# Fifth modulation vector moved behind the attention heads, and all six vectors on four column groups of TensorE

## The chip, the cores and the metric

The kernel runs on one NeuronCore of a Trainium2 chip. The metric is the device time of one execution in microseconds (us), the median of several runs; smaller is better. A profile is one further execution, recorded by the hardware profiler.

## The reference

Two layers (`DEPTH` = 2) of a backbone with model width 1024 run on 128 context tokens and 256 latent tokens, three tiles of 128 tokens. All is float32. What bears on the change is the modulation: two condition vectors (one for the context, one for the latent tokens) go through `silu` and a 1024 x 6144 matrix, and the six results of 1024 numbers each shift, scale and gate the layer.

```python
def modulation(cvec, w_mod_l, b_mod_l):
    m = jax.nn.silu(cvec) @ w_mod_l + b_mod_l
    return m.reshape(cvec.shape[0], 6, D_MODEL)

def trunk_layer(...):
    sh1, sc1, g1, sh2, sc2, g2 = [mod[:, i][:, None, :] for i in range(6)]
    h = rms_norm(x, n1) * (1.0 + sc1) + sh1
    proj = h @ w_in
    ...
    attn = block_attention(q, k_all, v_all)
    conv = conv_module(u, dw_w, dw_b, ln_g, ln_b)
    x = x + g1 * (jnp.concatenate([attn, conv], axis=-1) @ w_out)
    h2 = rms_norm(x, n2) * (1.0 + sc2) + sh2
    x = x + g2 * grouped_moe(h2, w_router, b_router, wg, wu, wd)
```

The vectors are counted from 0: vector 0 is `sh1`, vector 4 is `sc2` (the fifth), vector 5 is `g2`. Attention has 8 query heads and 2 key heads of width 64. The convolution has 31 taps on 512 channels (4 blocks of 128). The mixture has 16 experts.

## The kernel before, in words

Each engine has its program written out by hand (`block.tensor`, `block.vector`, `block.scalar`, `block.gpsimd`, `block.sync`), and the engines meet at semaphores. Nothing reorders the work: an engine does its instructions in the order of the code.

**Weights** come through a ring of eight slots of 2 MB in the tile `big`. SP issues all weight loads in one fixed order (`loads`), and each waits until TensorE has finished with what the slot held (`slot_used`). Per layer these are the vectors' weights (two pieces of 2 MB each), the input projection, the output projection, and three loads for each of 16 experts.

**A modulation vector** (`vector`, L1457) is eight steps k of the contraction. The stationary operand is `cs_rep[:, k, :]`, the two activated conditions repeated over 64 columns; the moving operand is one half (`LW` = 512 numbers) of the weight row. `LANES` = 2: one half goes to columns 0 to 63 of the array, the other to columns 64 to 127, so a vector is 16 matmuls of 64 columns x 512. The profile shows each float32 matmul as two records (and two weight loads), so a vector is 32 records. VectorE takes a vector out of PSUM (`mod_take`: L975 copies vectors 0 and 1, L979 adds the bias to 2, 3 and 5). `columns` (L1484) turns vectors 0 and 1 into columns by 16 small matmuls each. Vectors 2, 3, 4 and 5 are written to DRAM by GpSimd (`lane_out`, L323, one DMA for each lane) and read back broadcast to all partitions (`spread`, L547).

**Vector 4** goes another way: it is split over the eight heads (`HEAD_FILL`, `head_fill`, L1471). Every head has two of its 16 matmuls, with a stationary operand of 2 columns and 512 numbers moving; its first half (called 8) is done after head 3, its second (9) after head 7. VectorE takes each half with L983 and multiplies it by the gain of the second norm with L988, on two partitions. GpSimd writes it out with one DMA (L606).

**A head** on TensorE: for each tile the transposes of the probabilities (L1614) and the scores of the next head (L1590), then two matmuls of vector 4 (L1471), then probabilities times values (L1441, 128x64, 14 records). VectorE finds the maxima (L1176), does some convolution taps (L1102), and scales the head's output (L1182, L1184); ScalarE does the exponentials (L848) and takes the transposed probabilities (L855).

**The convolution's taps** are 124 VectorE instructions in one fixed order. `taps(n)` does the next n. The line that sets their places:

```python
EARLY_TAPS, ROPE_TAPS, BETWEEN_TAPS, LATE_TAPS, HEAD_TAPS = 80, 6, 6, 4, 4
```

80 come early, 6 inside each of the three rotary embeddings (`rope`; 6 after the first one in the second layer), 6 before `rope(1)`, 4 after vector 2 is taken: 108 ahead of the heads. The 16 that are left go 4 to a head, to heads 0 to 3.

**Behind the heads** TensorE transposes the convolution back (`conv_back`, L1601), transposes the heads' outputs (`mix_transposed`, L1647) and projects (`project_out`, L1662). Meanwhile the layer norm of the convolution runs through VectorE (L1192, L1197), GpSimd (L542, L543, L615, L616, L620) and ScalarE (L871). Its results let the second half of each `mix_transposed` go. Then comes the second norm, the router, the routing (VectorE, with vector 5 on TensorE beside it and, in the first layer, vectors 0 and 1 of the second), and the experts (L1746, L1762).

Of the kernel before, what the change touches and what calls it, by code (L numbers as in the profile page):

```python
# [5 lines left out]
ALU = mybir.AluOpType  # L6
# [30 lines left out]
LANES = 2  # L37
# [7 lines left out]
TAKES = [0, 1, 2, 3, 8, 9, 5]  # L45
# [81 lines left out]
EARLY_TAPS, ROPE_TAPS, BETWEEN_TAPS, LATE_TAPS, HEAD_TAPS = 80, 6, 6, 4, 4  # L127
# [100 lines left out]
def build(nc, x_prompt, x_sample, cache_k, cache_v, c, c_ctx, w_mod, b_mod, norm1_g, norm2_g, w_in, q_norm_g,  # L228
# [6 lines left out]
    with ExitStack() as ctx:  # L235
# [53 lines left out]
        assert o >= 5120 + 3 * LW  # L289
# [4 lines left out]
        sg = rowC = cut(CH)  # L294
# [67 lines left out]
        rowB_in = sem("rowB_in"); gain_in = sem("gain_in"); small_in = sem("small_in")  # L362
# [13 lines left out]
        mod_half_ps = sem("mod_half_ps")  # L376
# [152 lines left out]
        def _(pool):  # L529
# [25 lines left out]
            for l in range(LAYERS):  # L555
# [7 lines left out]
                pool.dma_start(rowS, b_mod[l:l + 1, 4 * D:5 * D].broadcast_to([2, D])).then_inc(rowB_in, 16)  # L563
# [34 lines left out]
                pool.wait_ge(modC_st, (l + 1) * 32)  # L598
# [30 lines left out]
                pool.wait_ge(modB_st, l * 48 + 48)  # L629
# [24 lines left out]
                pool.wait_ge(modG_st, (l + 1) * 32)  # L654
# [294 lines left out]
        def _(dve):  # L949
# [10 lines left out]
            def mod_take(l, c):  # L960

                bank = mod_bank(l, c)
                if c == 2:
                    dve.wait_ge(rowC_in, (l + 1) * 32)
                if c == 3:
                    dve.wait_ge(rowB_in, (l + 1) * 48)
                if c == 5:
                    dve.wait_ge(rowG_in, (l + 1) * 32)
                if c == 8:
                    dve.wait_ge(mod_half_ps, l + 1)  # L970
                else:
                    n = pieces(l, min(c, 4 if c == 9 else c))[-1][0]
                    dve.wait_ge(slot_used[slot_of(n)], uses(n))
# [3 lines left out]
                if c < 8:
                    row = (rowC[:, :], rowB, None, rowG)[c - 2]
                    v.tensor_tensor(row, ps[:, bank, :], row, ALU.add).then_inc(mod_taken, 1)  # L979
                else:  # L980
                    half = slice(c % 2 * SEG, (c % 2 + 1) * SEG)
                    row, gain = rowS[:, half], gainB[:, half]
                    v.tensor_tensor(row, ps[0:2, bank, :], row, ALU.add).then_inc(mod_taken, 1)  # L983
                if c in (8, 9):
                    if c == 8:
                        dve.wait_ge(gain_in, (l + 1) * 16)
# [42 lines left out]
            for l in range(LAYERS):  # L1029
# [142 lines left out]

# [258 lines left out]
        def _(pe):  # L1431
# [15 lines left out]
            def vector(l, j, k0=0, k1=KD):  # L1447

                for n, a, b in pieces(l, j):
                    for k in range(max(a, k0), min(b, k1)):  # L1450
# [5 lines left out]
                        for lane in range(LANES):  # L1456
                            mm = pe.matmul(ps[lane * LP:(lane + 1) * LP, mod_bank(l, j), :], cs_rep[:, k, :],  # L1457
                                           w[:, lane * LW:(lane + 1) * LW], start=(k == 0), stop=(k == KD - 1))
                        if k == b - 1:
                            mm.then_inc(slot_used[slot_of(n)], 1)  # L1460

            def head_fill(l, hd):

                c, k0, k1 = HEAD_FILL[hd]
                if k0 == 0:
                    pe.wait_ge(mod_taken, taken_at(l, 3 if c == 8 else 8))
                for n, a, b in pieces(l, 4):
                    for k in range(max(a, k0), min(b, k1)):
                        if c == 8 and k == a:
                            loaded(n)  # L1470
                        mm = pe.matmul(ps[0:2, mod_bank(l, c), :], cs_rep[:, k, 0:2],  # L1471
                                       slot_k(slot_of(n), b - a)[:, k - a, (c - 8) * SEG:(c - 7) * SEG],
                                       start=(k == 0), stop=(k == KD - 1))
                        if c == 8 and k == KD - 1:
                            mm.then_inc(mod_half_ps, 1)
                        if c == 9 and k == b - 1:
# [432 lines left out]
```

## Time and profile before

| what | us |
|---|---|
| runs: median (lowest to highest) of 3 | 1130.35 (1130.08 to 1140.29) |
| the profiled execution, its own time | 1134.84 |
| span in its trace | 1133.0 |
| TensorE busy in the span | 1003.9 (89%) |
| VectorE busy | 393.6 (35%) |
| granted TensorE clock, mean | 0.938 |

The span is the time from the first to the last instruction of the trace; the profiled execution's own time is 1.84 us longer. A granted clock of 1.00 is 2.4 GHz, 0.50 is 1.2 GHz. In the rows below PE is TensorE (PEld its weight loads), DVE is VectorE, ACT ScalarE, POOL GpSimd and SP the engine that issues the weight loads.

### The profile page before, as it was taken

Reading aid. Unit: us, or ns where it says so; the run is one execution under the profiler, and the core shown is the slowest. Engines: PE = TensorE matmul, PEld = TensorE weight load, DVE = VectorE, ACT = ScalarE, POOL = GpSimd, SP = SyncE. Lnnn points to the kernel's source line nnn. Section 1 sums busy time; section 2 is a strip of 40 time slices with the busy share of each in tenths; the row PEclk is TensorE's granted clock in tenths of the full one; section 3 lists DMA queues with packets and bytes.
Section 4 is the critical chain, followed back from the end, with each engine's and each line's share of the span. In section 5 each row is a group of like instructions: output and inputs, shape, how many; then the busy total and the mean of one; then the engine's idle time right before and its main releaser. Section 6 shows DMA issues by size and latency. Waiting matters only on the chain. (4 is left out here: it accounts for less than half of the span.)

```text
span 1133.0 us, 11425 instructions
## 1 busy us (share of the span) xinstructions
PE 1003.9 (89%) x4328; PEld 471.3 (42%) x4328; DVE 393.6 (35%) x857; ACT 152.3 (13%) x357; POOL 116.3 (10%) x176
## 2 busy tenths in 40 slices
PE   4799999999799998899899989999788888987993
PEld 1555544545233333333366534555433333333331
DVE  0159954334411111111035996434511111111106
ACT  1100144220000000000020014422000000000001
POOL 0100400501000000000111020050100000000001
PEclk9899989998899999999899999999689899999897
DMA  9926991259999996999980375235966999999814
GB/s 341 354 117 238 291 366 70 95 189 360 419 404 423 425 372 273 413 422 424 360 306 24 149 277 215 75 115 195 371 237 240 417 422 425 424 423 422 353 28 167
DMA packets 64406, 329.83 MB, mean 291 GB/s; under 512 B 6992, under 2 KB 9680, under 8 KB 47924
## 3 DMA queue, kind: packets, MB, share of 16 engines
q1 hardware_dynamic: 44224, 277.89, 61.2%
q0 software_dynamic: 8496, 28.68, 6.9%
q10 hardware_dynamic: 11588, 21.95, 5.9%
q8 instruction: 63, 1.03, 0.4%
q14 instruction: 35, 0.29, 0.1%
HBM read 306.67 MB, written 21.82 MB: 290 GB/s over the span
## 5 line engine op out<-in xcount | busy, mean ns | idle before, releaser
L1746 PE MATMUL ps<-big 128*64 128x512 f32 x1024 | 245.5, 631 | 29.0 <-DMA big<-in_w_up_dram 11.8
L1762 PE MATMUL ps<-big,scr 128*64 128x512 f32 x624 | 151.0, 623 | 5.3 <-DVE scr L1399 4.3
L1441 PE MATMUL ps<-big 128*128 128x384 f32 (+2 forms) x448 | 147.9, 492 | 5.2 <-ACT big L777 5.2
L1746 PEld LDWEIGHTS ps<-big 128*64 128x64 f32 x1024 | 81.7, 145 | 168.1 <-issue 157.1
L1102 DVE SCALAR_TENSOR_TENSOR scr<-scr,convw 128x384 f32<-128x384 f32 x240 | 134.0, 611 | 2.3
L1410 DVE TENSOR_TENSOR scr<-ps,scr 128x256 f32<-128x256 f32 x32 | 13.6, 425 | 315.5 <-ACT scr L932 315.5
L1441 PEld LDWEIGHTS ps<-big 128*128 128x128 f32 x448 | 86.0, 193 | 64.7 <-issue 24.6
L1457 PE MATMUL ps<-big,cs_rep 128*64 128x512 f32 x320 | 80.8, 656 | 14.0 <-DMA big<-in_w_mod_dram 14.0
L1762 PEld LDWEIGHTS ps<-big,scr 128*64 128x64 f32 x624 | 51.2, 143 | 91.1 <-issue 89.0
L1662 PE MATMUL ps<-big 128*128 128x512 f32 x192 | 84.4, 594 | 1.4 <-ACT big L817 1.4
L1746 PE MATMUL ps<-big,scr 128*64 128x512 f32 x224 | 51.3, 612 | 5.9 <-DVE scr L1388 5.9
L1662 PEld LDWEIGHTS ps<-big 128*128 128x128 f32 x192 | 35.7, 190 | 43.0 <-issue 41.1
L932 ACT ACTIVATE scr<-ps 128x256 f32<-128x256 f32 x32 | 12.3, 384 | 292.0 <-PE ps L1746 292.0
L1457 PEld LDWEIGHTS ps<-big,cs_rep 128*64 128x64 f32 x320 | 23.9, 151 | 59.1 <-issue 58.1
L644 POOL DMA_INDIRECT scr<-h_rows,slot_tok x16 | 15.4, 964 | 303.9 <-PE ps L1730 258.7
L1379 DVE COPY big<-ps 128x512 f32<-128x512 f32 x32 | 20.6, 686 | 47.8 <-PE ps L1730 47.8
L1590 PE MATMUL ps<-scr 64*128 64x384 f32 (+1 forms) x96 | 36.5, 468 | 0.0
L1441 PEld LDWEIGHTS ps<-scr 128*128 128x128 f32 x224 | 26.6, 194 | 14.7 <-issue 14.7
L894 ACT COPY scr<-ps 128x512 f32<-128x512 f32 x32 | 18.7, 586 | 101.5 <-PE ps L1762 101.5
L1755 PE MATMUL ps<-table_sb,scr 128*128 128x128 f32 x78 | 18.2, 315 | 15.4 <-DVE scr L1395 9.8
L1471 PE MATMUL ps<-big,cs_rep 128*2 128x512 f32 x64 | 31.7, 620 | 0.0
L1746 PEld LDWEIGHTS ps<-big,scr 128*64 128x64 f32 x224 | 15.9, 140 | 36.1 <-issue 29.3
(220 smaller groups left out, 819.7 us busy)
## 6 DMA issues: line engine op xcount, KB each, us to landing
big<-in_w_gate_dram SPq DMA_DIRECT2D x32, 2048.0 KB, 15.8
big<-in_w_up_dram SPq DMA_DIRECT2D x32, 2048.0 KB, 19.7
big<-in_w_down_dram SPq DMA_DIRECT2D x32, 2048.0 KB, 16.7
big<-in_w_mod_dram SPq DMA_DIRECT2D x23, 2048.0 KB, 15.5
big<-in_w_in_dram SPq DMA_DIRECT2D x6, 2048.0 KB, 26.8
expert_rows<-scr ACTq DMA_DIRECT2D x74, 128.0 KB, 8.2
big<-in_w_out_dram SPq DMA_DIRECT2D x4, 2048.0 KB, 15.6
expert_rows<-x ACTq DMA_DIRECT2D x1, 6912.0 KB, 42.0
```

The source lines that it names most:

```text
L644: pool.indirect_dma_start(out=xs[:, i % 2, :], out_offset=None, in_=h2_dram, in_offset=bass.IndirectOffsetOnAxis(ap=slot_tok[:, i * NT:i * ...
L894: a.copy(ybuf[:, j, :], ps[:, YB + j, :]).then_inc(y_taken, 1)
L1102: v.scalar_tensor_tensor(out, span, w, out, ALU.mult, ALU.add).then_inc(conv_step[m], 1)
L1379: ins = v.tensor_copy(hT[i % 2][:, 4 * b:4 * b + 4, :].rearrange("p k n -> p (k n)"), ps[:, XT + b, :])
L1441: mm = pe.matmul(out, stationary(k), moving(k), start=(k == 0), stop=(k == n - 1))
L1457: mm = pe.matmul(ps[lane * LP:(lane + 1) * LP, mod_bank(l, j), :], cs_rep[:, k, :], w[:, lane * LW:(lane + 1) * LW], start=(k == 0), stop= ...
L1471: mm = pe.matmul(ps[0:2, mod_bank(l, c), :], cs_rep[:, k, 0:2], slot_k(slot_of(n), b - a)[:, k - a, (c - 8) * SEG:(c - 7) * SEG], start=(k ...
L1590: pe.matmul(ps[:, 4 + t, 0:P * len(ks)], qT[g_ * HD:(g_ + 1) * HD, t, j * P:(j + 1) * P], kT[g_ * HD:(g_ + 1) * HD, ks[0] * P:(ks[-1] + 1) ...
L1662: mm = pe.matmul(ps[:, out_bank(t, n), :], hT[t][:, k, :], slot_w(s)[:, k, :], start=(k == 0), stop=(k == KD - 1))
L1746: mm = pe.matmul(ps[b * TT:(b + 1) * TT, bank, :].rearrange("p (m n) -> p m n", m=2), tokens(k), w[:, :, k, b * HF:(b + 1) * HF], start=(k ...
L1755: mm = pe.transpose(ps[:, bank, m * P:(m + 1) * P], rows[:, m:HF:2], ident)
L1762: mm = pe.matmul(ps[b * TT:(b + 1) * TT, bank, :], src[:, k % 2 * P + k // 2 * TT:k % 2 * P + (k // 2 + 1) * TT], w[:, k, b * SEG:(b + 1) ...
```

## The change

`LANES` becomes 4: a vector's weight row is cut into four quarters of 256 numbers, each on 32 columns of the array, so a vector is 32 matmuls of 32 columns x 256. This follows for all six vectors, for `columns` (32 small matmuls instead of 16) and for the DMAs of a lane, which are four instead of two. Vector 4 is now done like the others: `head_fill` is gone, the heads have no matmuls of it, and `vector(l, 4)` stands behind the last head, ahead of `conv_back`. VectorE takes it in one piece (128x256) and multiplies it by the gain, now spread over the same partitions. Its rows go out to DRAM with four DMAs in the midst of the layer norm on GpSimd; those of vector 3 go out earlier, as soon as it is taken. `BETWEEN_TAPS` falls from 6 to 2 and `LATE_TAPS` from 4 to 2, so by the diff 22 taps of a layer fall into the heads instead of 16 (four in each of heads 0 to 4, two in head 5).

```diff
-LANES = 2
+LANES = 4
...
-TAKES = [0, 1, 2, 3, 8, 9, 5]
+TAKES = [0, 1, 2, 3, 4, 5]
...
-EARLY_TAPS, ROPE_TAPS, BETWEEN_TAPS, LATE_TAPS, HEAD_TAPS = 80, 6, 6, 4, 4
+EARLY_TAPS, ROPE_TAPS, BETWEEN_TAPS, LATE_TAPS, HEAD_TAPS = 80, 6, 2, 2, 4
...
                 lane_in(pool, rowB, b_mod[l:l + 1, 3 * D:4 * D], rowB_in)
-                pool.dma_start(rowS, b_mod[l:l + 1, 4 * D:5 * D].broadcast_to([2, D])).then_inc(rowB_in, 16)
+                lane_in(pool, rowS, b_mod[l:l + 1, 4 * D:5 * D], rowB_in)
+                lane_in(pool, gainB, norm2_g[l:l + 1, :], rowB_in)
...
-                pool.wait_ge(slot_used[slot_of(("in", l, 3))], uses(("in", l, 3)))
-                pool.dma_start(gainB, norm2_g[l:l + 1, :].broadcast_to([2, D])).then_inc(gain_in, 16)
-
-                pool.wait_ge(mod_done, l + 1)
+                pool.wait_ge(mod_taken, taken_at(l, 3))
                 lane_out(pool, mod_dram[:, 3 * D:4 * D], rowB, modB_st)
-                pool.dma_start(mod_dram[:, 4 * D:5 * D], rowS).then_inc(modB_st, 16)
...
                     ln_affine(t)
                     if t:
                         ln_silu(t - 1)
+                    else:
+                        pool.wait_ge(mod_done, l + 1)
+                        lane_out(pool, mod_dram[:, 4 * D:5 * D], rowS, modB_st)
...
-                    if HEAD_FILL[hd][2] == KD:
-                        mod_take(l, HEAD_FILL[hd][0])
                     head_output(hd)
+                mod_take(l, 4)
                 ln_stats(0)
...
                         for lane in range(LANES):
-                            mm = pe.matmul(ps[lane * LP:(lane + 1) * LP, mod_bank(l, j), :], cs_rep[:, k, :],
+                            mm = pe.matmul(ps[lane * LP:(lane + 1) * LP, mod_bank(l, j), 0:LW], cs_rep[:, k, :],
                                            w[:, lane * LW:(lane + 1) * LW], start=(k == 0), stop=(k == KD - 1))
...
-                    head_fill(l, hd)
...
+                vector(l, 4)
                 for t in range(TILES):
                     conv_back(t)
...
-                    if n == 0:
-                        pe.wait_ge(mod_taken, taken_at(l, 9))
+                    if n == 2:
+                        pe.wait_ge(mod_taken, taken_at(l, 4))
```

TensorE, the last two heads of a layer and what follows, before (L1614 and L1590 are transposes and the next head's scores, L1441 probabilities times values, L1601 `conv_back`):

```order
L1614 MATMUL ps<-table_sb,scr 128x128
L1590 MATMUL ps<-scr 128x128
L1614 MATMUL ps<-table_sb,scr 128x128 x3
L1590 MATMUL ps<-scr 128x384
L1614 MATMUL ps<-table_sb,scr 128x128 x3
L1590 MATMUL ps<-scr 128x384
L1471 MATMUL ps<-big,cs_rep 2x512 x2
L1441 MATMUL ps<-scr 128x64 x7
L1614 MATMUL ps<-table_sb,scr 128x128 x7
L1471 MATMUL ps<-big,cs_rep 2x512 x2
L1441 MATMUL ps<-scr 128x64 x7
L1601 MATMUL ps<-table_sb,scr 128x128 x12
```

The same place in the changed kernel (its lines L1580, L1556, L1424 and L1567 are L1614, L1590, L1441 and L1601 of before; L1440 is `vector`):

```order
L1580 MATMUL ps<-table_sb,scr 128x128
L1556 MATMUL ps<-scr 128x128
L1580 MATMUL ps<-table_sb,scr 128x128 x3
L1556 MATMUL ps<-scr 128x384
L1580 MATMUL ps<-table_sb,scr 128x128 x3
L1556 MATMUL ps<-scr 128x384
L1424 MATMUL ps<-scr 128x64 x7
L1580 MATMUL ps<-table_sb,scr 128x128 x7
L1424 MATMUL ps<-scr 128x64 x7
L1440 MATMUL ps<-big,cs_rep 32x256 x32
L1567 MATMUL ps<-table_sb,scr 128x128 x12
```

The two 2x512 matmuls of each head are gone, and 32 matmuls of 32x256 stand between the last head and the transposes.

GpSimd from the writing out of vector 2 into the layer norm, before (L323 and L606 are DMAs to DRAM, L602 loads the gain, L542 to L616 are the layer norm):

```order
L323 DMA mod_rows<-scr 2x512 x2
L547 DMA gateB<-mod_rows 128x2x1024
L602 DMA big<-in_norm_g_dram 2x1024
L323 DMA mod_rows<-big 2x512 x2
L606 DMA mod_rows<-big 2x1024
L542 TENSOR_SCALAR stat<-stat 128x1
L543 TENSOR_TENSOR stat<-stat 128x1
L615 TENSOR_TENSOR big<-big,lnB 128x512
L616 TENSOR_TENSOR big<-big,lnB 128x512
L542 TENSOR_SCALAR stat<-stat 128x1
```

And in the changed kernel (L321 is `lane_out`, L539 to L610 the layer norm):

```order
L321 DMA mod_rows<-scr 2x256 x4
L544 DMA gateB<-mod_rows 128x2x1024
L321 DMA mod_rows<-big 2x256 x4
L539 TENSOR_SCALAR stat<-stat 128x1
L540 TENSOR_TENSOR stat<-stat 128x1
L609 TENSOR_TENSOR big<-big,lnB 128x512
L610 TENSOR_TENSOR big<-big,lnB 128x512
L321 DMA mod_rows<-big 2x256 x4
L539 TENSOR_SCALAR stat<-stat 128x1
```

Four DMAs of vector 4 now stand between the layer norm of tile 0 and that of tile 1; three that stood ahead of tile 0 are gone or moved to an earlier wait.

## Rows read from the trace of the kernel before

**Rows 1.** Page, the chain that ended last: shares by engine and by line

```profile
PE 28%; DMA 7%; DVE 3%; issue 1%; ACT 1%; POOL 0%; ACTq 0%; SPq 0%; DVEq 0%; POOLq 0%
PE ps L1746 10%; DMA big<-in_w_up_dram 5%; PE ps L1762 5%; PE ps L1662 4%; PE ps L1441 2%; PE ps L1590 1%; PE ps L1471 1%; PE ps L1457 1%; PE ps L1614 1%; DMA scr<-h_rows,slot_tok 1%; PE ps L1730 1%; PE ps L1755 0%; DMA scr<-expert_rows,pick_y 0%; DVE x L1016 0%; DVE x L1024 0%
```

**Rows 2.** Windows: one head of the second layer; its experts (columns in the first line)

```profile
core 0: us, PE busy (x) PEld busy (x) DVE busy (x) ACT busy (x) POOL busy (x), PEclk, DMA share, GB/s
698.25:704.93 6.68, 6.68 (x33) 3.46 (x33) 4.29 (x9) 2.82 (x11) 0.00 (x0) 1.00 0.00 0
...
900.00:910.00 10.00, 10.00 (x52) 3.66 (x50) 1.27 (x3) 0.97 (x2) 0.00 (x0) 1.00 1.02 427
```

**Rows 3.** The chain in order of time, second layer: one head, output projection (start, us, what)

```profile
698.25 1.81 PE ps L1471 x4
700.06 1.71 PE ps L1441 x14
...
704.93 1.81 PE ps L1471 x4
...
742.08 10.37 PE ps L1662 x24
```

**Rows 4.** Groups by line and form: busy us, mean ns of one; idle before

```profile
L1410 DVE TENSOR_TENSOR scr<-ps,scr 128x256 f32<-128x256 f32 x32 | 13.6, 425 | 315.5 <-ACT scr L932 315.5
...
L323 POOL DMA_DIRECT2D mod_rows<-scr x8 | 4.5, 572 | 10.7 <-DVE scr L979 10.7
```

**Rows 5.** Timeline, first layer's start (start, us, engine line op out<-in xcount [idle before])

```profile
39.66 7.09 PE L1457 MATMUL ps<-big,cs_rep 128*64 128x512 f32 x32
...
46.80 0.69 DVE L975 COPY scr<-ps 128x512 f32<-128x512 f32 x1 [16.98 <-PE ps L1457]
...
47.54 2.09 PE L1484 MATMUL ps<-table_sb,scr 128*64 128x2 f32 x32 [0.80 <-DVE scr L975]
```

**Rows 6.** Timeline, first layer, from the last projection to the heads

```profile
130.39 8.80 PE L1457 MATMUL ps<-big,cs_rep 128*64 128x512 f32 x40
...
142.37 0.28 DVE L1150 TENSOR_TENSOR scr<-scr 128x128 f32<-128x128 f32 x1
...
145.06 1.94 PE L1457 MATMUL ps<-big,cs_rep 128*64 128x512 f32 x8
```

**Rows 7.** Timeline, second layer, the same place

```profile
681.21 1.12 PE L1579 MATMUL ps<-table_sb,big 128*128 128x128 f32 x4 [5.73 <-DVE scr L1150]
...
682.47 2.82 PE L1457 MATMUL ps<-big,cs_rep 128*64 128x512 f32 x8
...
686.03 1.57 DVE L1176 TENSOR_REDUCE stat<-ps 128x1 f32<-128x128 f32 x3
```

**Rows 8.** Timeline, VectorE in one head of the second layer

```profile
698.76 2.57 DVE L1102 SCALAR_TENSOR_TENSOR scr<-scr,convw 128x384 f32<-128x384 f32 x4
701.80 0.18 DVE L1182 RECIPROCAL stat<-stat 128x3 f32<-128x3 f32 x1 [0.47 <-PE ps L1441]
```

**Rows 9.** Timeline, TensorE in the first head of the first layer

```profile
154.29 3.57 PE L1471 MATMUL ps<-big,cs_rep 128*2 128x512 f32 x4
157.79 2.17 PE L1441 MATMUL ps<-scr 128*128 128x64 f32 x14
```

**Rows 10.** Timeline, second layer behind the heads, GpSimd and TensorE

```profile
749.92 1.26 POOL L620 TENSOR_TENSOR big<-big,scr 128x512 f32<-128x512 f32 x1
...
752.28 0.60 PE L1647 MATMUL ps<-table_sb,big 128*128 128x128 f32 x4
```

**Rows 11.** Timeline, second layer's routing, TensorE and VectorE

```profile
800.04 7.20 PE L1457 MATMUL ps<-big,cs_rep 128*64 128x512 f32 x24
...
809.46 0.21 DVE L1286 TENSOR_TENSOR scr<-ps,scr 128x48 f32<-128x48 f32 x1 [4.74 <-PE ps L1441]
```

**Rows 12.** Windows: transposes behind the heads; first head of the first layer

```profile
739.00:742.00 3.00, 3.00 (x30) 2.94 (x29) 1.56 (x6) 0.76 (x2) 2.25 (x5) 1.00 0.78 289
...
152.00:158.00 6.00, 6.00 (x10) 1.43 (x11) 1.10 (x2) 2.08 (x7) 0.00 (x0) 0.50 1.04 402
```

More of the change, by code:

```diff
@@ L184, in mod_bank @@
         return 1
-    return {3: 0, 8: 0, 9: 0, 5: 3}[j]
+    return {3: 0, 4: 2, 5: 3}[j]
 def col_bank(l, s):
@@ L198, in taken_at @@
     return l * len(TAKES) + TAKES.index(j) + 1
-HEAD_FILL = [(8 + hd // 4, hd % 4 * (KD // 4), (hd % 4 + 1) * (KD // 4)) for hd in range(HEADS)]
 def qkv_bank(l, c, t):
@@ L288, in build @@
         zT = cut(CM * CONV_W).rearrange("p (m n) -> p m n", m=CM)
-        assert o >= 5120 + 3 * LW
+        assert o >= 6656
         qk_sq = scr[:, TILES * 640 + 2 * 640:2 * TILES * 640 + 2 * 640].rearrange("p (t n) -> p t n", t=TILES)
@@ L293, in build @@
         ck = cut(KVW)
-        sg = rowC = cut(CH)
+        sg = cut(CH)
+        rowC = sg[:, 0:LW]
         assert o <= 9832
@@ L308, in build @@
         colA = scr[:, 7168 + 2 * LW:7168 + 2 * LW + 3 * KD].rearrange("p (s k) -> p s k", k=KD)
-        rowB, rowS, rowG = scaleB[:, 0, 0:LW], shiftB[0:2, 0], scr[:, 6656:6656 + LW]
+        rowB, rowS, rowG = scaleB[:, 0, 0:LW], shiftB[:, 0, 0:LW], scr[:, 6656:6656 + LW]
         diag = h[:, :, 0:P]
-        gainB = hT[0][0:2].rearrange("p k n -> p (k n)")
+        gainB = shiftB[:, 0, LW:2 * LW]
         def lane_in(eng, rows, vec, done):
@@ L374, in build @@
         out_st = sem("out_st")
-        mod_half_ps = sem("mod_half_ps")
         convw_ps = sem("convw_ps"); hT_ps = sem("hT_ps"); proj_ps = sem("proj_ps"); conv_ps = sem("conv_ps")
@@ L653, in _ @@
                 lane_out(pool, mod_dram[:, 5 * D:6 * D], rowG, modG_st)
-                pool.wait_ge(modG_st, (l + 1) * 32)
+                pool.wait_ge(modG_st, (l + 1) * LANES * 16)
                 spread(gateB[:, :, :], 5, bcG_in)
@@ L963, in mod_take @@
                 if c == 2:
-                    dve.wait_ge(rowC_in, (l + 1) * 32)
+                    dve.wait_ge(rowC_in, (l + 1) * LANES * 16)
                 if c == 3:
-                    dve.wait_ge(rowB_in, (l + 1) * 48)
+                    dve.wait_ge(rowB_in, (l + 1) * 3 * LANES * 16)
                 if c == 5:
[L968 to L973, printed above, removed]
+                    dve.wait_ge(rowG_in, (l + 1) * LANES * 16)
+                n = pieces(l, c)[-1][0]
+                dve.wait_ge(slot_used[slot_of(n)], uses(n))
                 if c < 2:
-                    v.tensor_copy(rowA[:, c * LW:(c + 1) * LW], ps[:, bank, :]).then_inc(mod_taken, 1)
+                    v.tensor_copy(rowA[:, c * LW:(c + 1) * LW], ps[:, bank, 0:LW]).then_inc(mod_taken, 1)
                     return
[L977 to L986, printed above, removed]
+                row = (rowC, rowB, rowS, rowG)[c - 2]
+                v.tensor_tensor(row, ps[:, bank, 0:LW], row, ALU.add).then_inc(mod_taken, 1)
+                if c == 4:
                     dve.wait_ge(mod_taken, taken_at(l, c))
-                    ins = v.scalar_tensor_tensor(row, row, 1.0, gain, ALU.add, ALU.mult)
-                    if c != 8:
-                        ins.then_inc(mod_done, 1)
+                    v.scalar_tensor_tensor(row, row, 1.0, gainB, ALU.add, ALU.mult).then_inc(mod_done, 1)
             def columns(l):
@@ L1456, in vector @@
                         for lane in range(LANES):
-                            mm = pe.matmul(ps[lane * LP:(lane + 1) * LP, mod_bank(l, j), :], cs_rep[:, k, :],
+                            mm = pe.matmul(ps[lane * LP:(lane + 1) * LP, mod_bank(l, j), 0:LW], cs_rep[:, k, :],
                                            w[:, lane * LW:(lane + 1) * LW], start=(k == 0), stop=(k == KD - 1))
                         if k == b - 1:
[L1460 to L1476, printed above, removed]
                             mm.then_inc(slot_used[slot_of(n)], 1)
```

6 lines of the change are left out of this document (3 added, 3 removed).

## Prediction

> **What bounds the kernel now.** I read the page's chain first, then the windows of single stages, then the chain in order of time and the timelines around each edit. The chain that ended last is TensorE's far more than DMA's, and L1471 and L1457, the two places of the vectors, both stand on it [rows 1]. The windows show two kinds of stage. In a head TensorE is busy 6.68 of 6.68 us, VectorE 4.29, DMA not at all: TensorE is the bound. Among the experts the DMA share is 1.02 at 427 GB/s: weights are the bound there [rows 2]. A weight load starts when TensorE frees its slot, so I expect a stage that ends sooner ahead of the experts to start their stream sooner by as much. The chain goes from the matmuls of a head's filling (L1471, 1.81 us) straight into probabilities times values, and comes round every 704.93 - 698.25 = 6.68 us [rows 3]. Filling is therefore on the path, not in a gap.
>
> **Price of a vector on four column groups.** No row of before has four groups. A full-width record of 512 numbers takes 10.37 / 24 = 0.432 us [rows 3]. On two groups 32 records take 7.09 us [rows 5], 0.443 for a pair: two groups ran at the price of one. If four do, a vector is 8 steps x 2 passes x half of 0.432 = 3.5 us. If only two ever run together, 64 half-length records come to 6.9; one after another, to 13.8. In between stands the rate at which records follow each other: 32 tiny ones of L1484 take 2.09 us, 65 ns each [rows 5], and 64 at that rate make 4.2 us. Those carry 64 stationary columns and the new ones carry 32, so I take 3.5, nearest to the pair's row, and keep 4.2 and 6.9 as bounds; 13.8 I leave out, since it would need the pair's overlap to vanish.
>
> That pairs of groups cost 0.443 against 0.432 leaves 3% for packing [rows 3, 5]. The Trainium skill ("TensorE: Matmul & The Clock Gate", Part 3, measured speedup) speaks against a clean factor of four: three column tiles gave 2.38 and four row tiles 3.07. With 3.07 an estimate is 8 x 4 x 0.432 / 3.07 = 4.5 us a vector, and the sum below would be some 3.5 us less.
>
> **Start.** Layer 0's second vector lies bare on the chain: 7.09 to 3.5, -3.6. The copy out of PSUM behind it takes 0.69 for 128x512 [rows 5]; 128x256 takes 0.43 [rows 4]: -0.26. `columns` has twice the records with half the columns; I take 0 (bounds 0 and +2.1, the whole of L1484 again [rows 5]). GpSimd's extra DMAs lie beside the loads. Together -3.9.
>
> **Ahead of the heads, layer 0.** From 130.39 TensorE does 40 records, then three pieces of 8, and is free for the scores at 145.06 + 1.94 = 147.0 [rows 6]. With vectors at half the price its own work would end 7 us sooner, but the last piece follows the third rotary embedding on VectorE, which ends at 142.65 [rows 6]. Ahead of that four taps go (BETWEEN 6 to 2), each about 2.57 / 4 = 0.64 in a dense row [rows 8] and I take 0.61: -2.4. GpSimd issues vector 2's bias with four DMAs instead of two, 0.57 each [rows 4], which can push its part of the embedding about 1 later. So it ends between 140.2 and 141.2; behind it stand the transposes (682.47 - 681.21 = 1.26 in the same place of layer 1 [rows 7]) and a piece of half of 1.94. Scores start at 142.4 to 143.4 rather than at 147.0; I take -4.3, nearer to the early end since the DMAs only partly delay it (bounds -3 and -5.5).
>
> **Ahead of the heads, layer 1.** Here TensorE already waits 5.73 us for the embedding, then does 2.82 us of vector 3 before the scores [rows 7]. The taps give -2.4, the pieces behind 2.82 to about 1.4 and their take a little: -4.0.
>
> **Heads.** Without filling the period is 6.68 - 1.81 = 4.87. VectorE has 4.29 busy in that period [rows 2] and waited 0.47 ahead of the output's scaling [rows 8], so it is nearly the bound, but not quite; heads with taps were four a layer and become six. Their 2.57 us [rows 8] lie beside TensorE. If that cover is gone in the twelve heads with taps, 0.3 us each make +3.6 as the bound. Layer 0: its first head ran cold, with 3.57 us for filling [rows 9]; 6 x 1.81 + 3.5 + 1.3 (the last head keeps a wait on ScalarE that filling covered) = -15.7. Layer 1: 7 x 1.81 + 1.3 = -14.0.
>
> **Vector 4 behind the heads.** Nothing stands beside it: +3.5 in each layer. VectorE's layer norm is queued behind its take, but that needs the transposes which follow the vector on TensorE anyway.
>
> **GpSimd's four DMAs in the layer norm.** They stand between tile 0 and tile 1, 4 x 0.57 = 2.3 us [rows 4], against three taken from ahead of tile 0, where GpSimd was waiting. Tile 1's last step ends at 749.92 + 1.26 = 751.18, and the transposes that need it start at 752.28 [rows 10]: 1.1 us of slack. What is over, about 1.25, becomes a wait of TensorE; with the later take and the next tile's transposes I count +2.2 in each layer (bounds 0 and +4.6, twice the DMAs).
>
> **Routing.** In layer 1 vector 5 holds TensorE for 7.20 us from 800.04, and VectorE then waits 4.74 for the small matmul behind it [rows 11]. At 3.5 the vector is done before the masks (ready 4.74 - 2.18 = 2.6 us before it is): -2.8 with the shorter take. In layer 0 the routing's matmuls are followed by weight-bound experts: -0.5 (bounds 0 and -3).
>
> **Sum.** -3.9 -4.3 -15.7 +3.5 +2.2 -0.5 (layer 0: -14.8 behind the start) -4.0 -14.0 +3.5 +2.2 -2.8 (layer 1: -15.1) = -33.8. The profiled execution's own 1134.84 becomes 1101.0. It stands 4.5 above the median of the runs, 1130.35, so the forecast is 1097 on the median's scale. Its own range: vectors at 4.2 cost 0.7 at four bare places, +2.8; GpSimd's bound +4.8; taps uncovered +3.6; and downward GpSimd -4.4 and routing -2.5. They hardly all fall together: 1091 to 1104.
>
> **Rivals.**
> (A) Four groups don't run together, only two. Then the vectors remain at 7: start -0.3, ahead of the heads -0.5 and -3.0, heads -29.7, vector 4 +7.0 a layer, GpSimd +2.2 a layer, routing -0.3. That is -15.4, 1115. For it: no row has more than two groups. Against: the pair costs 0.443, so groups don't share a stream [rows 3, 5]. Chance 0.12.
> (B) The clock falls in heads without filling, and the kernel is slower. Filling is the only part of a head with long streams. The first head of layer 0 shows the price at 1.2 GHz (granted clock 0.50 in its window [rows 12]): filling 3.57 against 1.81, probabilities times values 2.17 against 1.71 [rows 3, 9]. About 3.2 us of a 4.87 period stream and stretch by 1.9: 3.2 x 1.9 + 1.7 = 7.8 to 8.1, so a head costs 3.2 over the forecast. Fifteen heads +48 and the cold vector 4 +3.5 a layer: -33.8 + 55 = +21, 1151. It decides from about ten cold heads on. For it: the window at 0.50 is a head. Against: 739 to 742 is nearly nothing but transposes, and its granted clock is 1.00 [rows 12]; and heads without filling leave hardly any gap on TensorE. Chance 0.07.
>
> That window of transposes at 1.00 [rows 12] is at odds with the Trainium skill ("TensorE: Matmul & The Clock Gate", Part 4), which says that transposes don't count as busy for the clock; by that rule (B) would be the likely case.
>
> (C) Layer 0's gain doesn't get through its experts: the loads ahead of them can't begin sooner, since DMA is full [rows 2]. Then some -15 of -33.8 are given back, and the time is 1112 to 1116. For it: the share of 1.02. Against: in the heads the DMA stands at 0.00 [rows 2], the slots being full, so the stream begins when TensorE frees one. Chance 0.07.
> (D) The change does what it says, but VectorE with 22 taps becomes the bound of the heads and GpSimd's DMAs of the layer norm: +3.6 and +4.8 in full, 1105 to 1107. Chance 0.08.
>
> **How the numbers follow.** Forecast 0.66, A 0.12, B 0.07, C 0.07, D 0.08. The range of 8 in 10 holds the forecast with its bounds, D, C and most of A: 1089 to 1117. What a measurement of this kernel can tell from no change is about 1%, 11 us. Within it fall only a half A with C together, or a B that stops after about ten heads: 0.04. Slower: 0.07, which is B. Faster by over 1%: 0.89.
>
> **What would show it.** In the changed profile: a vector's 64 records in about 3.5 us behind the last head (6.9 speaks for A); a head's period of 4.87 with no idle time on TensorE ahead of probabilities times values (idle put down to VectorE speaks for D); a granted clock of 1.00 in the heads (0.50 is B); a wait of one to two us at the first of the second transposes put down to ScalarE behind GpSimd; the first expert of layer 0 some 18 to 19 us sooner (the same distance at the end of layer 0's experts, else C). The forecast is wrong if the vector takes 7 us, if the heads' period stays over 5.3, or if the clock falls.

## The result, and the profile after

The changed kernel takes 1152.05 us (median of 4 runs, 1150.05 to 1159.38), against 1130.72 for the kernel before beside it: a ratio of 1.0187 with a 95% interval of 1.015 to 1.0225. It is slower by about 2%, where 1097 was forecast.

First the page of the changed kernel: the busy times, and of its 40 slices the line of the granted clock in tenths.

```profile
PE 1004.8 (87%) x4840; PEld 500.3 (43%) x4840; DVE 386.8 (34%) x853; ACT 152.6 (13%) x357; POOL 136.2 (12%) x218
PEclk9899855898899999998899975579879989999997
```

TensorE has no less to do than before (1003.9 us then), although all the filling is gone. Two dents stand in the clock, 5 5 in slices 6 and 7 and 5 5 in slices 25 and 26. These are the heads of the two layers, and the windows there answer to [rows 2]:

```profile
137.00:139.00 2.00, 1.57 (x6) 0.69 (x5) 1.57 (x4) 1.29 (x2) 0.00 (x0) 1.00 1.05 385
...
160.00:180.00 20.00, 20.00 (x60) 12.32 (x59) 9.21 (x19) 6.43 (x22) 0.00 (x0) 0.50 0.01 3
...
208.00:212.00 4.00, 4.00 (x62) 2.44 (x52) 0.97 (x3) 0.00 (x0) 0.00 (x0) 0.94 0.42 120
...
700.00:720.00 20.00, 20.00 (x61) 12.32 (x59) 8.85 (x19) 6.12 (x19) 0.00 (x0) 0.50 0.01 1
```

TensorE is busy 20.00 of 20.00 us at a granted clock of 0.50, 1.2 GHz. In layer 0 the clock had fallen in a wait of 2.70 us, stood at 1.00 again at the first scores (137 to 139 us) and fell once more in the first head; in layer 1 it had fallen ahead of the scores, where TensorE waits 2.58 and 6.55 us for rotary embeddings. Only behind the heads, in vector 4, does it return to 2.4 GHz. The chain in order of time, second layer, answers to [rows 3]; its last two lines are vector 4 and GpSimd's DMAs of it:

```profile
696.12 3.18 PE ps L1424 x14
...
705.05 3.18 PE ps L1424 x14
...
757.23 5.75 PE ps L1440 x64
...
769.88 1.50 POOL mod_rows L321 x3
```

A head comes round every 705.05 - 696.12 = 8.93 us, against 6.68 with filling and 4.87 forecast without. Probabilities times values take 3.18 instead of 1.71: the same work at half the clock.

TensorE's timeline answers to [rows 5, 6, 9, 10]:

```profile
37.51 3.66 PE L1440 MATMUL ps<-big,cs_rep 128*32 128x256 f32 x64
...
122.94 4.52 PE L1440 MATMUL ps<-big,cs_rep 128*32 128x256 f32 x80
...
133.67 1.12 PE L1545 MATMUL ps<-table_sb,big 128*128 128x128 f32 x4 [2.70 <-DVE scr L1135]
...
139.51 0.33 PE L1580 MATMUL ps<-table_sb,scr 128*128 128x128 f32 x1 [0.93 <-ACT scr L845]
...
206.08 4.83 PE L1440 MATMUL ps<-big,cs_rep 128*32 128x256 f32 x64
...
777.11 0.66 PE L1613 MATMUL ps<-table_sb,big 128*128 128x128 f32 x4 [1.04 <-POOL big L614]
```

A vector on four groups takes 3.66 us at full clock, where 3.5 was forecast: four groups do run together (80 records in 4.52 us, 56.5 ns each). Behind the heads the vector starts at low clock and takes 4.83 and 5.75. TensorE now waits 2.70 us for a rotary embedding in layer 0, where its longer vectors covered that wait before. The wait behind GpSimd, forecast at one to two us, is 1.04 us in layer 1.

The table compares each stretch with the kernel before, in us, by the starts in TensorE's timelines. The last column is an experiment below, in which the clock rises in the first head.

| from ... to | forecast | the change | vector 4 in head 0 |
|---|---|---|---|
| start to layer 0's scores | -8.2 | -10.1 | -9.5 |
| heads and vector 4, layer 0 | -12.2 | +16.8 | -11.0 |
| behind the heads to the router's transposes | +2.2 | +2.2 | +2.7 |
| router to the first expert | -0.5 | -2.9 | -2.9 |
| experts to layer 1's first transposes | 0 | -1.3 | -3.8 |
| on to layer 1's scores | -4.0 | -3.0 | -3.0 |
| heads and vector 4, layer 1 | -10.5 | +22.0 | -6.3 |
| behind the heads to the router's transposes | +2.2 | +3.0 | +3.4 |
| router to the first expert | -2.8 | -2.4 | -2.5 |
| experts to the end | 0 | -5.6 | -2.3 |
| sum (span) | -33.8 | +18.6 | -35.3 |

All of the loss is in two rows, the heads: +38.8 where -22.7 was forecast. The other rows add up to -20.2 for -11.1. The largest single part that wasn't forecast, -5.6 from the experts to the end, no run explains.

### The profile page after: what moved, and what is told of

The parts are those of the page before. It is cut to its first block and busy times, and to the rows that moved or that the text cites. A ratio compares the mean times of both kernels' runs of the same rounds, so it can differ in the third digit from the quotient of the medians.

```text
span 1151.6 us, 12483 instructions
## 1 busy us (share of the span) xinstructions
PE 1004.8 (87%) x4840; PEld 500.3 (43%) x4840; DVE 386.8 (34%) x853; ACT 152.6 (13%) x357; POOL 136.2 (12%) x218
## 5 line engine op out<-in xcount | busy, mean ns | idle before, releaser
L1728 PE MATMUL ps<-big,scr 128*64 128x512 f32 x624 | 148.5, 618 | 5.3 <-DVE scr L1382 4.3
L1424 PE MATMUL ps<-big 128*128 128x384 f32 (+2 forms) x448 | 147.2, 491 | 5.1 <-ACT big L774 5.1
L1424 PEld LDWEIGHTS ps<-big 128*128 128x128 f32 x448 | 85.6, 192 | 64.4 <-issue 24.0
L1728 PEld LDWEIGHTS ps<-big,scr 128*64 128x64 f32 x624 | 49.4, 142 | 91.4 <-issue 90.5
L1440 PE MATMUL ps<-big,cs_rep 128*32 128x256 f32 x768 | 57.5, 457 | 15.0 <-DMA big<-in_w_mod_dram 15.0
L1556 PE MATMUL ps<-scr 64*128 64x384 f32 (+1 forms) x96 | 62.0, 754 | 0.0
L1424 PEld LDWEIGHTS ps<-scr 128*128 128x128 f32 x224 | 49.0, 330 | 15.1 <-issue 12.9
L1712 PE MATMUL ps<-big,scr 128*64 128x512 f32 x224 | 49.6, 595 | 5.9 <-DVE scr L1371 5.9
L1424 PE MATMUL ps<-scr 128*128 128x64 f32 x224 | 51.6, 423 | 0.0
L1440 PEld LDWEIGHTS ps<-big,cs_rep 128*32 128x32 f32 x768 | 26.6, 129 | 38.9 <-issue 26.5
L1160 DVE TENSOR_REDUCE stat<-ps 128x1 f32<-128x384 f32 (+1 forms) x48 | 22.5, 468 | 59.9 <-PE ps L1556 59.8
L1580 PE MATMUL ps<-table_sb,scr 128*128 128x128 f32 x112 | 34.4, 432 | 0.9 <-ACT scr L845 0.9
L1696 PE MATMUL ps<-table_sb,scr 128*128 128x128 f32 x128 | 20.1, 305 | 17.3 <-DMA scr<-h_rows,slot_tok 17.3
## 6 DMA issues: line engine op xcount, KB each, us to landing
big<-in_w_in_dram SPq DMA_DIRECT2D x6, 2048.0 KB, 24.5
```

Of the source, the lines that this page charges most:

```text
L1160: v.tensor_reduce(stats(NM + TILES * (hd % 2) + t), ps[:, 4 + t, 0:P * len(KEY_CHUNKS[t])], AX.X, ALU.max, negate=True).then_inc(nmax, 1)
L1424: mm = pe.matmul(out, stationary(k), moving(k), start=(k == 0), stop=(k == n - 1))
L1556: pe.matmul(ps[:, 4 + t, 0:P * len(ks)], qT[g_ * HD:(g_ + 1) * HD, t, j * P:(j + 1) * P], kT[g_ * HD:(g_ + 1) * HD, ks[0] * P:(ks[-1] + 1) ...
L1580: mm = pe.transpose(ps[:, 1 + t, n * P:(n + 1) * P], prob[:, t, n * P:(n + 1) * P], ident)
L1696: mm = pe.transpose(ps[:, XT + m // 4, m % 4 * P:(m % 4 + 1) * P], xs[:, i % 2, m::KD], ident)
L1712: mm = pe.matmul(ps[b * TT:(b + 1) * TT, bank, :].rearrange("p (m n) -> p m n", m=2), tokens(k), w[:, :, k, b * HF:(b + 1) * HF], start=(k ...
```

## The experiments

The theory after the result: a TensorE whose clock is low at the first head, or falls in it, stays low, because a head without filling has only transposes and short matmuls; the long streams of the filling had lifted it. Rivals: the four groups or the moved taps slow the heads, GpSimd's DMAs do, or the place of vector 4's weight slots decides.

**Only the move of vector 4** (two column groups, taps where they were):

```diff
-LANES = 4
+LANES = 2
-EARLY_TAPS, ROPE_TAPS, BETWEEN_TAPS, LATE_TAPS, HEAD_TAPS = 80, 6, 2, 2, 4
+EARLY_TAPS, ROPE_TAPS, BETWEEN_TAPS, LATE_TAPS, HEAD_TAPS = 80, 6, 6, 4, 4
```

> The change with two column groups and the taps where they were: only vector 4 moves behind the heads. Theory 1 (the filling held TensorE's clock up): granted clock 0.50 in the heads of both layers, head period 8.9 us, vector 4 cold at about 9 to 11 us, time 1160 to 1175. Theory 2 (the four groups or the moved taps slow the heads): clock 1.00, period about 4.9, vector 4 at 7.1, time 1110 to 1120.

Measured: 1147.40 us, ratio 1.014 (1.0086 to 1.0195). Its windows, and TensorE's timeline at the first head of either layer:

```profile
142.00:148.00 6.00, 4.82 (x23) 2.14 (x21) 3.98 (x9) 3.57 (x8) 1.45 (x4) 1.00 1.05 388
...
160.00:200.00 40.00, 40.00 (x123) 25.87 (x124) 15.45 (x33) 13.33 (x43) 0.00 (x0) 0.50 0.12 48
...
706.00:709.00 3.00, 1.81 (x8) 0.81 (x7) 2.79 (x6) 2.20 (x6) 0.91 (x2) 1.00 0.97 355
...
720.00:740.00 20.00, 20.00 (x112) 13.02 (x111) 12.44 (x32) 11.33 (x37) 0.00 (x0) 1.00 0.00 1
```

```profile
147.30 0.33 PE L1580 MATMUL ps<-table_sb,scr 128*128 128x128 f32 x1 [1.18 <-ACT scr L845]
...
708.59 0.33 PE L1580 MATMUL ps<-table_sb,scr 128*128 128x128 f32 x1 [1.19 <-ACT scr L845]
```

The time lies outside both ranges, and each theory was met in one layer: the same heads ran at 0.50 in layer 0 and at 1.00 in layer 1. From the scores to the transposes behind the heads layer 0 takes 77.7 us and layer 1 46.8, against 57.2 and 54.1 before. The clock at the entrance isn't what differs, since it is 1.00 in both; in layer 1 it had fallen in a wait of 5.72 us, and a piece of vector 3 (2.75 us) lifted it just ahead of the scores. Nor is it the wait for ScalarE's first exponentials, 1.18 and 1.19 us: the clock fell behind it in layer 0 and held in layer 1. What decides between the two remains open. Shown is that heads without filling can keep a clock of 1.00 to the last one, and that neither the four groups nor the taps are needed for the loss.

**Only the four groups** (the kernel before with `LANES = 4` for all vectors but vector 4, which stays as filling):

> The kernel before with four column groups for vectors 0, 1, 2, 3 and 5; vector 4 stays in the heads as filling, the taps stay. Theory 1: heads as before, period 6.68 at clock 1.00, vectors at 3.6 us, gain from the start (3.9), ahead of the heads (2 to 4 a layer) and routing (up to 3.3): 1115 to 1122. Theory 2: the four groups cost as much as they bring, 1128 to 1135.

Measured: 1131.81 us, ratio 0.9985 (0.995 to 1.0021): nothing, a miss for theory 1's number. In its profile layer 0's first expert starts 6.8 us sooner (283.69 against 290.46), so the vectors did gain. One part that is lost again shows in the windows ahead of layer 1's heads:

```profile
660.00:690.00 30.00, 18.87 (x129) 8.91 (x122) 24.60 (x49) 7.65 (x20) 9.69 (x12) 0.69 1.03 400
690.00:700.00 10.00, 10.00 (x46) 4.92 (x44) 4.27 (x9) 2.98 (x11) 0.00 (x0) 0.92 0.09 35
```

Shorter vectors leave TensorE idle longer (busy 18.87 of 30, 23.08 before), the clock is 0.69 instead of 0.94 (0.76 if the 30 us are laid as far from the scores as before), and layer 1's heads take 57.3 us instead of 54.1, since the clock rises only in the first head's filling. Another part, 3.1 us, is lost between layer 0's first expert and layer 1's first transposes; the border between the layers is taken up below.

**All of vector 4 in the first head**:

```diff
+                    if hd == 0:
+                        vector(l, 4)
                     if hd:
                         pe.wait_ge(attn_out, l * HEADS + hd)
...
-                vector(l, 4)
                 for t in range(TILES):
                     conv_back(t)
...
```

The vector also goes to another PSUM bank, and the wait for its take moves with it.

> The change, but all of vector 4 (64 records on four groups) stands in the first head of each layer, where the filling stood; heads 1 to 7 have none. Theory 1a (a cold TensorE stays cold without long streams, a warm one stays warm): the vector lifts the clock in head 0, heads 1 to 7 run at 1.00 with a period of about 4.9, time 1090 to 1105. Theory 1b (heads without filling also bring a warm clock down): clock back to 0.50 within the heads, period 8.9 in most, time 1135 to 1150.

Measured: 1101.27 us, ratio 0.9747 (0.9694 to 0.98). Its windows in layer 0, and TensorE's timeline there:

```profile
141.00:145.00 4.00, 4.00 (x10) 1.75 (x9) 1.73 (x4) 1.80 (x8) 2.76 (x5) 0.50 1.05 385
145.00:150.00 5.00, 5.00 (x65) 2.27 (x64) 0.56 (x1) 1.17 (x4) 0.00 (x0) 0.71 1.04 399
150.00:155.00 5.00, 5.00 (x35) 3.20 (x27) 1.34 (x4) 1.35 (x4) 0.00 (x0) 1.00 1.03 406
...
175.00:180.00 5.00, 5.00 (x31) 3.33 (x30) 3.15 (x8) 2.95 (x11) 0.00 (x0) 1.00 0.00 0
```

```profile
145.56 4.76 PE L1440 MATMUL ps<-big,cs_rep 128*32 128x256 f32 x64
150.26 1.77 PE L1424 MATMUL ps<-scr 128*128 128x64 f32 x14
...
155.12 1.77 PE L1424 MATMUL ps<-scr 128*128 128x64 f32 x14
```

The clock rises within the vector and stays at 1.00 through seven heads that have no filling. They come round every 4.87 us (150.26, 155.12, 160.00), as forecast. Theory 1a holds.

**One step of vector 4 in each head** (the same place, `vector(l, 4, hd, hd + 1)` in every head):

> The change, but each head does one of the eight steps of vector 4 on four groups (8 records, 0.45 us at full clock, against 1.81 us of filling before). Theory 1a: if so little holds and lifts the clock, period about 5.4 and time 1090 to 1105. Theory 1b: too little, clock 0.50, period about 9.8, time 1148 to 1160.

Measured: 1163.13 us, ratio 1.0299 (1.0245 to 1.0352), theory 1b. TensorE's timeline in layer 0:

```profile
162.81 1.08 PE L1440 MATMUL ps<-big,cs_rep 128*32 128x256 f32 x8
163.82 3.25 PE L1424 MATMUL ps<-scr 128*128 128x64 f32 x14
...
172.75 1.08 PE L1440 MATMUL ps<-big,cs_rep 128*32 128x256 f32 x8
```

The period is 9.94 us: the same vector, cut into eight pieces of 1.08 us at low clock, lifted nothing, where one piece of 4.76 did.

**The stream in head 0 as work that is thrown away**, vector 4 behind the heads as in the change. The added matmuls repeat vector 4 into a bank that isn't read:

```diff
...
+                    if hd == 0:
+                        stream(l)
```

> The change as it is, vector 4 behind the heads, but in the first head of each layer TensorE does the 64 records of vector 4 once more into a bank that nothing reads. Theory 1a (the clock alone decides): heads 1 to 7 at 1.00 with a period of 4.87, vector 4 behind them at 3.6 us; against the run with all of vector 4 in head 0 (1101) one vector a layer more, 1106 to 1112. Theory 3 (that run gained because vector 4's two slots come free earlier and two expert loads start 35 us sooner): clock 1.00, but 1118 to 1135.

Measured: 1112.43 us, ratio 0.9811 (0.9779 to 0.9844). Its window behind the stream in layer 0:

```profile
152.00:190.00 38.00, 38.00 (x268) 26.03 (x269) 23.83 (x55) 19.45 (x60) 0.76 (x2) 1.00 0.32 121
```

Added work of some 5 us a layer makes the change 40 us faster. That is 0.4 over the range of theory 1a and 6 under that of theory 3: slots that come free sooner aren't needed for the gain.

**Vector 4 ahead of the heads**, in the wait for the third embedding, taken by VectorE before head 0 and stored by GpSimd during the heads:

```diff
                 for t in range(TILES):
+                    if t == 2:
+                        vector(l, 4)
                     pe.wait_ge(rope_ready, l * 3 + t + 1)
...
```

> The change, but vector 4 stands ahead of the heads, where TensorE waits 2.7 us (layer 0) and 5.8 us (layer 1) for the third rotary embedding; VectorE takes it ahead of head 0 and GpSimd stores it during the heads. No head has a long stream. If TensorE enters the heads warm and the first head's short waits don't bring the clock down: period 4.87 from the start, layer norm without the four DMAs, 1085 to 1095. If the clock falls in the first head's short waits it stays down for the layer: 33 us a layer, 1115 to 1125 with one layer cold, 1140 to 1155 with both.

Measured: four runs far apart, 1148.45, 1120.03, 1151.64 and 1147.21 us; the mean granted clock was 0.903 in the one at 1120 and 0.878 to 0.880 in the others, against 0.93 before. Windows, and TensorE's timeline, of the one at 1148.45:

```profile
140.00:145.00 5.00, 4.16 (x56) 2.40 (x57) 0.43 (x2) 1.07 (x2) 0.76 (x1) 1.00 1.06 389
145.00:150.00 5.00, 4.08 (x14) 1.87 (x13) 4.52 (x11) 3.50 (x9) 4.00 (x8) 0.87 1.03 393
150.00:160.00 10.00, 10.00 (x31) 6.20 (x30) 2.36 (x6) 3.42 (x11) 0.00 (x0) 0.50 1.03 406
```

```profile
135.60 3.32 PE L1439 MATMUL ps<-big,cs_rep 128*32 128x256 f32 x32 [3.68 <-DMA big<-in_w_mod_dram]
140.79 1.93 PE L1439 MATMUL ps<-big,cs_rep 128*32 128x256 f32 x32 [1.86 <-DMA big<-in_w_mod_dram]
...
147.17 0.33 PE L1583 MATMUL ps<-table_sb,scr 128*128 128x128 f32 x1 [0.92 <-ACT scr L844]
...
149.54 0.90 PE L1583 MATMUL ps<-table_sb,scr 128*128 128x128 f32 x3
```

Here TensorE waits 3.68 and 1.86 us for vector 4's weights, enters the heads at 1.00, waits 0.92 us for ScalarE's first exponentials, and its clock falls to 0.50 within the first head; it stays there to the last, in both layers. The time of this execution, 1148, lies in the range given for both layers cold. The one at 1120 lies in the range for one, but it has no profile, so that isn't shown. A long stream ahead of the first head thus didn't keep the clock up here. That the wait of 0.92 us is what brought it down isn't shown: in the run with only the move, 1.18 us did in one layer and 1.19 us didn't in the other.

**The store of vector 4 during the heads** (from here on with vector 4 in head 0): VectorE takes it in head 6, and GpSimd's four DMAs follow those of vector 3.

```diff
+                    if hd == 6:
+                        mod_take(l, 4)
                     head_output(hd)
-                mod_take(l, 4)
...
                 lane_out(pool, mod_dram[:, 3 * D:4 * D], rowB, modB_st)
+                pool.wait_ge(mod_done, l + 1)
+                lane_out(pool, mod_dram[:, 4 * D:5 * D], rowS, modB_st)
...
-                    else:
-                        pool.wait_ge(mod_done, l + 1)
-                        lane_out(pool, mod_dram[:, 4 * D:5 * D], rowS, modB_st)
```

> As the run with all of vector 4 in head 0 (1101), but VectorE takes it in head 6 and GpSimd writes its four lanes to DRAM during the heads instead of between the layer norm of tiles 0 and 1. If the four DMAs cost what I put on them (2.2 us a layer, and 2.7 and 3.4 more measured from the transposes to the router's): 4 to 7 us less, 1094 to 1097. If the wait behind them is hidden or replaced by another: 1100 to 1102.

Measured: 1097.34 us, ratio 0.9664 (0.9641 to 0.9686). GpSimd's and TensorE's timelines, layer 0:

```profile
182.97 1.98 POOL L321 DMA_DIRECT2D mod_rows<-big  x4 [37.61 <-DVE big L974]
```

```profile
198.41 0.60 PE L1614 MATMUL ps<-table_sb,big 128*128 128x128 f32 x4
...
203.22 0.60 PE L1614 MATMUL ps<-table_sb,big 128*128 128x128 f32 x4
```

The waits for GpSimd are gone. From the transposes behind the heads to the router's it is 39.29 us in layer 0 and 39.28 in layer 1, as in the kernel before (39.30 and 39.29): the price of the four DMAs, with the later take, was the 2.7 and 3.4 of the table, and it is given back in full.

**The layer border.** With four groups the turning of vectors 0 and 1 into columns is 128 records. TensorE's timeline in the run with only the four groups:

```profile
536.82 2.17 PE L1485 MATMUL ps<-table_sb,scr 128*32 128x2 f32 x128 [0.73 <-ACT scr L895]
544.41 8.98 PE L1747 MATMUL ps<-big 128*64 128x512 f32 x32 [5.42 <-issue]
```

Two column groups for the second layer's vectors 0 and 1, on top of vector 4 in head 0:

```diff
+def lanes(l, j):
+    return 2 if l and j < 2 else LANES
...
-                        for lane in range(LANES):
+                        for lane in range(lanes(l, j)):
...
```

> As the run with all of vector 4 in head 0 (1101), but the second layer's vectors 0 and 1 are back on two column groups, so the turning into columns at the layer border is 64 records instead of 128. With four groups the 128 records took 2.2 us and TensorE then waited 5.4 us without a releaser in the profile, 64 took 4.0 with 0.7 behind them: if that wait comes from the number of instructions, 2 to 4 us less, 1097 to 1099. If it comes from the weights that are still on their way: 1100 to 1103.

Measured: 1103.87 us, ratio 0.9715 (0.9687 to 0.9742). The place in the timeline of the run with vector 4 in head 0, and in this one's:

```profile
520.98 9.93 PE L1713 MATMUL ps<-big 128*64 128x512 f32 x32 [5.00 <-DMA big<-in_w_up_dram]
```

```profile
520.09 4.01 PE L1459 MATMUL ps<-table_sb,scr 128*64 128x2 f32 x64 [0.73 <-ACT scr L896]
524.94 9.69 PE L1722 MATMUL ps<-big 128*64 128x512 f32 x32 [0.85 <-issue]
```

The wait went from 5.00 to 0.85 us, and the time didn't tell it: 0.9715 and 0.9747 have intervals that overlap, and 1103.87 is nearer to the range expected if that wait is for weights than to the other. Both together with the early store:

> The early store and the second layer's vectors 0 and 1 on two column groups together. The border measured alone moved nothing I could tell (1104 against 1101, on another chip): if it costs 0 to 3 us, 1097 to 1100; if fewer instructions at the border do help and the chip hid it, 1093 to 1096.

Measured: 1097.33 us, ratio 0.9687 (0.9657 to 0.9717), as the early store alone. One profile puts that wait down to the load of an expert's weights, the others to nothing that they show. What it is remains open; removing it gains nothing that could be measured.

**The six taps back ahead of the heads** (early store, `BETWEEN_TAPS` 6, `LATE_TAPS` 4):

> As the run with the early store (1097, 0.966 of before), but the six taps a layer are back ahead of the heads (BETWEEN 6, LATE 4). If VectorE bounds the way into the heads, as I priced the move (2.4 us a layer): 4 to 6 us more, 1101 to 1104. If the two taps of LATE and the longer heads hide it: 1096 to 1099.

Measured: 1099.78 us, ratio 0.9724 (0.9687 to 0.976). In its profile TensorE waits 4.81 us for layer 0's last embedding, against 2.70 with the taps moved: 2.1 of the 2.4 that I priced are there. In the time a price of 2 or 3 us is likely and not shown: the interval just misses that of the early store (0.9641 to 0.9686) and overlaps that of the run with both (0.9657 to 0.9717), which is the same up to the layer border.

**Vector 4 in two halves**, the first ahead of head 0's wait for ScalarE, the second where the whole stood (early store):

> As the run with the early store, but vector 4 is cut in two in the first head: steps 0 to 3 ahead of the wait for the first exponentials (0.9 us of idle TensorE), steps 4 to 7 where the whole vector stood. If either half lifts the clock: 1 to 3 us less a layer, 1091 to 1096. If half a vector isn't enough at that place, heads at 0.50 in one or both layers: 1125 to 1160.

Measured: 1094.45 us, ratio 0.9686 (0.9631 to 0.9741), runs from 1088.16 to 1103.93. TensorE's timeline in layer 0:

```profile
142.00 2.85 PE L1440 MATMUL ps<-big,cs_rep 128*32 128x256 f32 x32
144.79 0.33 PE L1580 MATMUL ps<-table_sb,scr 128*128 128x128 f32 x1
...
148.09 1.93 PE L1440 MATMUL ps<-big,cs_rep 128*32 128x256 f32 x32
```

The first half lifts the clock and fills the wait (no idle time stands at 144.79). The median is 3 us under the early store's, the ratio not: a gain isn't shown.

**Vector 4 in the fourth head** (early store, `hd == 3` for `hd == 0`), to see whether the stream or the place does it:

> As the run with the early store (1097), but the 64 records of vector 4 stand in the fourth head of each layer instead of the first. If they are what lifts the clock: heads 0 to 2 at 0.50 with a period of 8.93, heads 4 to 7 at 1.00 with 4.87; three heads cold instead of one cost about 12 us a layer (3 x 4.06), 1117 to 1124. If the clock recovers by itself after some heads, or VectorE's taps in heads 0 to 4 matter: 1095 to 1105; if the place at the start of the heads is what counts, heads 4 to 7 cold as well: 1145 to 1160.

Measured: 1121.41 us, ratio 0.9914 (0.9877 to 0.9952). TensorE's timeline in layer 1, and the windows of layer 0:

```profile
689.54 3.25 PE L1424 MATMUL ps<-scr 128*128 128x64 f32 x14
...
698.46 3.25 PE L1424 MATMUL ps<-scr 128*128 128x64 f32 x14
...
707.39 5.91 PE L1440 MATMUL ps<-big,cs_rep 128*32 128x256 f32 x64
713.23 1.78 PE L1424 MATMUL ps<-scr 128*128 128x64 f32 x14
```

```profile
170.00:176.00 6.00, 6.00 (x38) 2.57 (x41) 3.50 (x6) 2.07 (x7) 0.00 (x0) 0.50 0.00 0
176.00:182.00 6.00, 6.00 (x65) 3.77 (x56) 1.12 (x4) 0.74 (x2) 0.00 (x0) 0.99 0.75 254
```

The period is 8.92 us up to the stream, the same matmuls take 3.25 before it and 1.78 behind it, and the time is 24 us over that with the stream in head 0, as three cold heads a layer ask. That settles the cause: the stream lifts the clock in each place that was tried from the first head on, and heads that have fallen to 1.2 GHz stay there until it comes.

## Why the prediction was wrong

The step that failed is the choice between the forecast and rival (B), in (B)'s line "Against". With it fell the heads' term of the sum: -15.7 and -14.0 stand on a period of 4.87 us at full clock, and the change runs at 1.2 GHz with a period of 8.93. The line's two reasons were a window of transposes at 1.00 [rows 12] and that "heads without filling leave hardly any gap on TensorE". The window showed 3 us behind a TensorE that was already at full clock; it could say that transposes leave a high clock alone there, not that they raise a low one. And no gap isn't enough: the changed kernel's TensorE is busy 20.00 of 20.00 us at 0.50. The row that decided was on record as well: layer 0's first head at 0.50 [rows 12], whose filling took 3.57 us [rows 9] and was followed by heads at full clock, as a window of before behind that filling shows:

```profile
160.00:164.00 4.00, 4.00 (x16) 1.76 (x16) 2.18 (x6) 2.39 (x8) 0.00 (x0) 1.00 1.02 409
```

I booked its 3.5 us as a gain from dropping it, and didn't ask what it did for the heads behind it.

Rival (B)'s time, 1151, is what came (1152), and part of that is luck. Its heads at 7.8 to 8.1 us assumed that only 3.2 us of the period stretch. All of it does, by 8.93 / 4.87 = 1.83, and in all sixteen heads, where (B) counted fifteen. Against that its cold vector 4, +3.5 a layer, was too dear (4.83 and 5.75 against 3.66 are +1.2 and +2.1), and the rows outside the heads gained 9 us more than forecast.

The other terms, by the run in which the clock rises in head 0:

- Four groups at 3.5 us a vector: 3.66 measured; the bounds 4.2 and 6.9 weren't needed, (A) is out. The estimate from the figure for four row tiles of the Trainium skill ("TensorE: Matmul & The Clock Gate", Part 3) was 4.5; the trace differs and decides. Four quarter rows take 4 x 56.5 = 226 ns, where one alone would take 216 (half of 0.432 us), a factor of 3.8.
- `columns` at 0: its 64 records took 1.18 us in layer 0, where 32 had taken 2.09.
- A head of 4.87 with 22 taps: met; VectorE kept up with no wait of TensorE on it, which takes out that half of (D).
- The gain of the heads: -11.0 in layer 0 for -12.2, but -6.3 in layer 1 for -10.5. The first head is cold in both layers once vectors are shorter, which the forecast had only for layer 0, in the kernel before.
- GpSimd's four DMAs: +2.7 and +3.4 for +2.2 a layer; moving them gave both back. Right in mechanism and 1.7 us too small in all, of the 4.8 that (D) put on it.
- Routing in layer 0: -2.9 for -0.5 (its bound was -3); in layer 1 -2.5 for -2.8.
- Layer 0's gain goes through the experts: 20.7 us sooner at the first expert, 24.5 at the next layer's first transposes. (C) is out.
- The sum, -33.8, is -35.3 in that run's span, and that is luck in part: its heads gained 5.4 us less than forecast, and its experts gained 6.1 (-3.8 and -2.3) that weren't forecast and that no run explains.

The Trainium skill ("TensorE: Matmul & The Clock Gate", Part 4) says that transposes don't count as busy for the clock in the way that other matmuls do. I weighed it against the window at 1.00 and put it aside. The runs agree with it in that heads of transposes and short matmuls didn't raise a clock of 0.50, in any of the sixteen heads of the change; the same heads kept a clock of 1.00 for seven in a row with vector 4 in head 0.

Of the changed parts, then: the four groups gain in the stretches where they stand (alone, with the filling kept, no gain in the time was shown), the store in the layer norm costs some 6 us of span, the taps gain some 2 us a layer at the entrance that the time doesn't show, and taking the long streams out of the first head costs about 50 (1152 against 1101). The version with vector 4 in head 0 and the early store, 1097 us or 0.9664 of before, is faster than both kernels.

## What to carry to other kernels

Work that looks like filler may hold the clock: before it is taken out of a stage of transposes and short matmuls, look at the granted clock at that stage's entrance and through its first instructions, and at which instruction it rises. An entrance at full clock isn't enough: in layer 0 it fell within the first head. A window at full clock proves nothing about a stage that stands at half clock; take the row where the clock rose as the evidence. One long stream behind the last wait at the entrance did here what filling in all eight heads did, at a third of the price (4.8 us against 8 x 1.81).

## What the runs showed of the hardware that was not expected

- Identical heads, with TensorE busy all the time, ran at 0.50 in one layer and at 1.00 in the other, in one execution, though both layers were entered at 1.00 and had the same wait in the first head (the run with only the move: 1.18 and 1.19 us).
- A full clock was lost behind such a short wait even after long work: in layer 0 of that run the clock stood at 1.00 and TensorE was busy up to the wait of 1.18 us, and the heads then ran at 0.50.
- A short stream doesn't do the same each time. In the change a piece of 1.94 us stands just ahead of the scores in both layers, at low clock; in layer 0 the granted clock was 1.00 behind it (137 to 139 us), in layer 1 it stayed at 0.50.
- Small matmuls can follow each other far faster than the 65 ns of [rows 5]: 128 records of 32 stationary columns took 2.17 us, 17 ns each.
